# Norm sums in column groups, a narrow reciprocal spread by matmuls, and an earlier place for the filter spectra

## The reference

```python
def rmsnorm(x, g):
    xf = x.astype(jnp.float32)
    y = xf * lax.rsqrt(jnp.mean(xf * xf, axis=-1, keepdims=True) + EPS)
    return (y * g.astype(jnp.float32)).astype(x.dtype)

h = modulate(rmsnorm(x, norm1_g[l]), shift, scale)     # h * (1 + scale) + shift
P = h @ w_in[l]       # q, k, v, the Hyena inputs and two gates
# then attention, Hyena, merge, w_o; x += gate1 * ...
h = modulate(rmsnorm(x, norm2_g[l]), shift2, scale2)
# layer 0: dense SwiGLU (ffn_w1, ffn_w3, ffn_w2); layer 1: top-2 of 8 experts
```

## Time and profile before

| what | value |
|---|---|
| median of three runs | 1837.5 us |
| profiled execution, its own time | 1836.34 us |
| span of the profiled execution | 1834.5 us |
| mean granted TensorE clock | 0.988 |
| TensorE matmul busy | 1766.9 us, 96% of the span |
| VectorE, ScalarE, GpSimd busy | 38%, 23%, 3% |

### The profile page before, as it was taken

The page is one execution under the profiler, slowest core; times in us unless marked ns, Lnnn a source line. Parts: engine busy times, 40 slices in busy tenths (PEclk is TensorE's granted clock), DMA queues, the critical chain, the costliest instruction groups (busy, mean ns, idle before and its releaser), DMA issues.

```text
span 1834.5 us, 41948 instructions
## 1 busy us (share of the span) xinstructions
PE 1766.9 (96%) x19374; PEld 1398.8 (76%) x19374; DVE 696.2 (38%) x950; ACT 423.4 (23%) x582; POOL 52.9 (3%) x61
## 2 busy tenths in 40 slices
PE   7999999999999999998998999999999999999997
PEld 3777676786788888877877886778679997677775
DVE  5457656444433335978745552010100010101013
ACT  4233344332422222215324441000000000000001
POOL 0000000002000001210000010000000000000000
PEclk9999999999999999999999999999999999999998
DMA  9721311235122225773331389999999999999991
GB/s 390 298 93 46 108 58 47 69 117 221 69 91 91 91 96 205 254 293 113 126 108 70 138 352 367 382 418 403 389 398 405 411 405 400 374 405 399 420 410 68
DMA packets 66414, 440.26 MB, mean 240 GB/s; under 512 B 7537, under 2 KB 7793, under 8 KB 22850
## 3 DMA queue, kind: packets, MB, share of 16 engines
q1 hardware_dynamic: 60482, 404.19, 56.4%
q0 software_dynamic: 4976, 30.70, 4.5%
q10 hardware_dynamic: 784, 2.75, 0.4%
HBM read 433.81 MB, written 3.80 MB: 239 GB/s over the span
## 4 chain that ended last, share of the span: by engine, by line
PE 89%; DVE 6%; ACT 2%; issue 2%; DMA 0%; DVEq 0%; ACTq 0%; SPq 0%
PE psum L2082 25%; PE psum L1601 14%; PE psum L1603 13%; PE psum L1602 13%; PE psum L2103 12%; PE psum L1648 1%; PE psum L1840 1%; PE psum L1862 1%; ACT units_hi L632 1%; PE psum L2058 1%; DVE units_lo L1005 1%; PE psum L1631 1%; PE psum L1822 1%; PE psum L1823 1%; PE psum L1824 1%
## 5 line engine op out<-in xcount | busy, mean ns | idle before, releaser
L2082 PE MATMUL psum<-expert_units,gathered 128*32 128x256 f32 (+1 forms) x9216 | 469.0, 361 | 3.8 <-issue 3.5
L2082 PEld LDWEIGHTS psum<-expert_units,gathered 128*32 128x32 f32 x9216 | 366.0, 110 | 99.4 <-issue 6.6
L1601 PE MATMUL psum<-h_hi,units_hi 128*128 128x512 f32 (+1 forms) x928 | 344.7, 371 | 10.9 <-DVE h_lo L1076 5.3
L1603 PE MATMUL psum<-h_hi,units_lo 128*128 128x512 f32 (+1 forms) x928 | 336.6, 363 | 0.0
L1602 PE MATMUL psum<-h_lo,units_hi 128*128 128x512 f32 (+1 forms) x928 | 336.5, 363 | 0.0
L1005 DVE TENSOR_TENSOR units_lo<-raw_units,units_hi 128x2048 fp32r<-128x2048 f32 (+2 forms) x88 | 175.2, 1991 | 265.9 <-ACT units_hi L632 265.9
L632 ACT ACTIVATE units_hi<-raw_units 128x2048 fp32r<-128x2048 f32 (+2 forms) x88 | 147.2, 1673 | 406.3 <-PE psum L1603 351.3
L2103 PE MATMUL psum<-expert_units,expert_midT 128*32 128x256 f32 x4080 | 229.6, 379 | 0.1
L1601 PEld LDWEIGHTS psum<-h_hi,units_hi 128*128 128x128 f32 x928 | 176.9, 191 | 50.8 <-issue 22.4
L2103 PEld LDWEIGHTS psum<-expert_units,expert_midT 128*32 128x32 f32 x4080 | 172.5, 110 | 50.5 <-issue 2.3
L1603 PEld LDWEIGHTS psum<-h_hi,units_lo 128*128 128x128 f32 x928 | 176.8, 191 | 27.4
(11 more groups left out here) (307 smaller groups left out, 1688.5 us busy)
## 6 DMA issues: line engine op xcount, KB each, us to landing
expert_units<-in_moe_up SPq DMA_DIRECT2D x128, 1024.0 KB, 9.9
expert_units<-in_moe_w SPq DMA_DIRECT2D x88, 1024.0 KB, 9.7
expert_units<-in_moe_up_rest SPq DMA_DIRECT2D x64, 768.0 KB, 7.6
raw_units<-in_w_in SPq DMA_DIRECT2D x40, 1024.0 KB, 4.8
raw_units<-in_ffn_w SPq DMA_DIRECT2D x22, 1024.0 KB, 4.8
mod_units<-in_w_mod_rows POOLq DMA_DIRECT2D x20, 1024.0 KB, 6.2
raw_units<-in_ffn_w SPq DMA_DIRECT2D x16, 704.0 KB, 5.4
raw_units<-in_w_pab SPq DMA_DIRECT2D x16, 512.0 KB, 3.3
```

The costliest lines, as they stand in the source:

```text
L1601: MM(o, wh, xh, start=first, stop=False)
L1603: return MM(o, wl, xh, start=False, stop=last)
L2082: ins = MM(o[GRP * q:GRP * (q + 1), :], G[:, k, at, GRP * rr:GRP * (rr + 1)], W[:, kk, q, :], start=k == 0 and rr % 2 == 0, stop=k == DK - ...
```

## The change

Each norm sum becomes four matmuls with 32 columns of ones, one in each column group of TensorE. Group g sums a quarter of the tokens, so that PSUM rows 32g to 32g+31 hold the sums of quarter g in 128 columns (64 for q = 3). Root and reciprocal run over these 128 (64) columns. Four further matmuls (`norm_spread`) have a broadcast column of the identity as weights and lay row 32g over all 128 rows, for quarter g; ScalarE copies the result to `rs` (`norm_rows`). Whoever read `rs` after the reciprocal now waits for `n_rs`.

The order changes too. At the start sums 6 and 7 go ahead of the taps, the spread follows the taps, the first scale trip precedes all spectra, and all eight spectra precede the shift trip. VectorE's reciprocal goes ahead of the tap decays. ScalarE copies four spectra before unit 0's high part, and makes unit 1's after 12 of the 16 norm items. Only the 64 rows of `hy_w3` that layer 0 needs are loaded (256 KB in place of 512 KB). The two modulation trips after `w_o` are cut: two units before sums 6 and 7, two after them, then the spread.

```diff
@@ ScalarE
-                A(rs[:, c0:TOK], PS[:, 7, c0:TOK], ACT.Sqrt, bias=eps[:, 0:1], scale=1.0 / D).then_inc(n_rt, 1)
+                A(rs[:, norm_part(q, 0, c0)], PS[:, 7, norm_part(q, 0)], ACT.Sqrt, bias=eps[:, 0:1], scale=1.0 / D).then_inc(n_rt, 1)
+
+            def norm_rows(q):
+                c0 = norm_c0[q]
+                act.wait_ge(n_spread, q + 1)
+                A(rs[:, c0:TOK], PS[:, 7, c0:TOK], ACT.Copy).then_inc(n_rs, 1)
...
                     norm_root(0)
-                    for q in range(5):
+                    norm_rows(0)
+                    for q in range(4):
                         spectrum_out(0, q)
                     hi(0, 0, 0)
-                    for q in range(5, 7):
-                        spectrum_out(0, q)
-                    hi(1, 1, 0)
-                    early = 7
+                    early = 4
...
                     norm_root(2)
-                    for q in range(2, 5):
+                    for q in range(2, 4):
                         spectrum_out(l, q)
+                    norm_rows(2)
+                    spectrum_out(l, 4)
                     early = 5
...
+                else:
+                    norm_hi(0, SHIFT1, HH, 0, 12)
+                    hi(1, 1, 0)
+                    norm_hi(0, SHIFT1, HH, 12, 4)
@@ VectorE
-                link(V_.reciprocal(rs[:, c0:TOK], rs[:, c0:TOK]))
+                V_.reciprocal(rs[:, norm_part(q, 0, c0)], rs[:, norm_part(q, 0, c0)]).then_inc(n_rec, 1)
...
-                    decayed(0)
                     norm_reciprocal(0)
                     dve.wait_ge(consts_in, 16)
+                    decayed(0)
@@ TensorE
-                    MM(PS[:, 7, c0:TOK], ones[:], sq[:, k % 2, c0:TOK], start=k == 0, stop=k == DK - 1).then_inc(n_pe, 1)
+                    for g in range(4):
+                        last = MM(PS[GRP * g:GRP * (g + 1), 7, norm_part(q, 0)], ones[:, 0:GRP], sq[:, k % 2, norm_part(q, g, c0)],
+                                  start=k == 0, stop=k == DK - 1, skip_group_check=True)
+                    last.then_inc(n_pe, 1)
+
+            def norm_spread(q):
+                c0 = norm_c0[q]
+                pe.wait_ge(n_rec, q + 1)
+                for g in range(4):
+                    last = MM(PS[:, 7, norm_part(q, g, c0)], ident[:, GRP * g:GRP * g + 1].to_broadcast([P, P]), rs[:, norm_part(q, 0, c0)],
+                              start=True, stop=True)
+                last.then_inc(n_spread, 1)
...
+                    if l and q == 4:
+                        norm_spread(2)
                     if bank == 7:
-                        pe.wait_ge(n_rt, 2 * l + 1)
+                        pe.wait_ge(n_rs, 2 * l + 1)
...
+            norm_sums(0, range(6, DK))
             filter_taps(0)
-            norm_sums(0, range(6, DK))
-            filter_spectra(0, 0, 2)
+            norm_spread(0)
             pe.wait_ge(s_ready, 1)
             mod_units(0, 0)
-            filter_spectra(0, 2, 3)
+            filter_spectra(0, 0, 2)
             mod_turn(0, 0)
-            filter_spectra(0, 3, 6)
+            filter_spectra(0, 2)
             mod_units(0, 1)
-            filter_spectra(0, 6, 7)
             mod_turn(0, 1)
-            filter_spectra(0, 7)
...
+                mod_units(l, MTRIPS - 1, 0, 2)
                 norm_sums(2 * l + 1, (DK - 2, DK - 1))
+                mod_units(l, MTRIPS - 1, 2)
+                norm_spread(2 * l + 1)
                 if l == 0:
-                    mod_units(0, LATE_TRIP)
...
-            mod_units(1, MTRIPS - 1)
-            pe.wait_ge(n_rt, 4)
```

More of the change, by code:

```diff
@@ L314, in build @@
         n_sq, n_pe, n_rt = sem("n_sq"), sem("n_pe"), sem("n_rt")
+        n_rec, n_spread, n_rs = sem("n_reciprocal"), sem("n_spread"), sem("n_rs")
         n_add = sem("n_add")
@@ L378, in build, with norm_part @@
         pooled = [0, 6, 6, 6, 0, 0]
+        def norm_part(q, g, c0=0):
+            w = (TOK - norm_c0[q]) // 4
+            return slice(c0 + g * w, c0 + (g + 1) * w)
         adds_before = [sum(c - 1 for c in pooled[:q] if c) for q in range(6)]
@@ L732, in _ @@
                     spectrum_out(l, q)
-                    norm_hi(2 * l, SHIFT1, HH, 2 * (q - early), 2)
-                norm_hi(2 * l, SHIFT1, HH, 2 * (8 - early), DK if l else 2 * DK)
+                    if l:
+                        norm_hi(2, SHIFT1, HH, 2 * (q - early), 2)
+                if l:
+                    norm_hi(2, SHIFT1, HH, 2 * (8 - early), DK)
+                else:
+                    norm_hi(0, SHIFT1, HH, 0, 12)
+                    hi(1, 1, 0)
+                    norm_hi(0, SHIFT1, HH, 12, 4)
                 for n in range(U_U):
@@ L857, in _ @@
                 norm_root(2 * l + 1)
+                norm_rows(2 * l + 1)
                 if l == 0:
@@ L1079, in norm_lo @@
                 end = len(todo) if end is None else end
+                dve.wait_ge(n_rs, q + 1)
                 for j in range(first, end):
@@ L1627, in norm_sums, with mod_units @@
                         pe.wait_ge(n_add, adds_before[q] + pooled[q] - 1)
-                        MM(PS[:, 7, c0:TOK], ones[:], square_sum(q), start=True, stop=False).then_inc(n_pe, pooled[q])
+                        for g in range(4):
+                            last = MM(PS[GRP * g:GRP * (g + 1), 7, norm_part(q, 0)], ones[:, 0:GRP], square_sum(q)[:, norm_part(q, g)],
+                                      start=True, stop=False, skip_group_check=True)
+                        last.then_inc(n_pe, pooled[q])
                         continue
                     pe.wait_ge(n_sq, 8 * q + k + 1)
-                    MM(PS[:, 7, c0:TOK], ones[:], sq[:, k % 2, c0:TOK], start=k == 0, stop=k == DK - 1).then_inc(n_pe, 1)
-            def mod_units(l, i):
-                if l or i:
+                    for g in range(4):
[5 more added lines that the diff above has]
+                pe.wait_ge(n_rec, q + 1)
+                for g in range(4):
+                    last = MM(PS[:, 7, norm_part(q, g, c0)], ident[:, GRP * g:GRP * g + 1].to_broadcast([P, P]), rs[:, norm_part(q, 0, c0)],
+                              start=True, stop=True)
+                last.then_inc(n_spread, 1)
+            def mod_units(l, i, first=0, end=MRING):
+                if (l or i) and first == 0:
                     pe.wait_ge(md_row, trip(l, i))
                 rows = P // MRING
-                for u in range(MRING):
+                for u in range(first, end):
                     if l:
```

3 lines of the change are left out of this document (2 added, 1 removed).

## The result

The changed kernel takes 1842.79 us (median of 20 runs, 1839.52 to 1849.77), the kernel before 1839.47 us (20 runs, 1834.91 to 1843.32) in the same rounds. The ratio on record is 1.0028, 95% interval 1.0019 to 1.0036; it is not the quotient of the two medians, which is 1.0018. By the ratio the changed kernel is 5.2 us slower, by the medians 3.3 us, where the forecast was 3.9 us faster and its range ended at 1837.2 us. The profiled execution of the changed kernel took 1841.88 us (span 1840.1, before 1834.5), and TensorE still holds the chain of waits.

The account below looks back on a forecast made before the run. TensorE, holding 89% of the chain of waits, was taken to bound the kernel. Start -3.4, second norm -1.6, third 0 and fourth +1.1 gave -3.9 us, so 1832.4 profiled and 1833.6 median, range 1829.6 to 1837.2.

Parts of the forecast that it names:

- The start: First norm up to the first product: short sums and new order bring -3.4 us, product near 43.1 against 46.10.
- T: End of the taps at the start: 23.3 us forecast, 21.7 if never slow, about 25 if slow throughout.
- T + 18.9: Start of the first product, 18.9 us after the taps end: 42.2 us before any allowance for slow matmuls.
- the 0.9 added for slow matmuls there: Spread or scale trip after the one-column tap matmuls: 0.9 us for slow matmuls, first product at 43.1.
- a possible 1.6 us: Taps at the start: holes left by short sums make TensorE slow until half way, +1.6 us.
- Rival (b): Start: clock low throughout the taps and part of the trip; T near 25, product 45.5, total -1.1, 1836.4 us; chance 0.27.
- The second norm: Second norm: earlier sums and narrow reciprocal let VectorE start at 455.35 in place of 456.99, -1.6 us.
- The third: Third norm: -0.3 from down projection sums, +0.3 from the later last spectrum copy, sum 0.
- The fourth: Fourth norm: half trip and spread between sum and copy delay VectorE's first block and the router matmuls, +1.1 us.
- rival (c): Norm sums: column groups do not overlap, each sum costs 0.86 us and spreads come on top; 1837.5 us, chance 0.06.
- the row bound: Narrow norm sum: a record every 54 ns if the weight load binds, up to 0.43 us a sum.
- Rival (d): First product stays at 1.2 GHz for all 48 matmuls, 10 us more; with other gains +4.5, 1842 us; chance 0.06.

Follow-up runs that it names:

- e2_wide_sums: Changed kernel, new order kept, but first norm with 128-column sums, wide root and reciprocal, no spread; ratio 0.9992 to the kernel before.
- e3_fill: Changed kernel, narrow sums kept, plus eight extra 128x128 matmuls with unused result among the first norm's sums; ratio 0.9992 to the kernel before.
- e7_second_only: Kernel before with only the second norm made narrow as in the changed kernel; ratio 0.9987 to the kernel before.
- e10_first_expert: e2_wide_sums plus 80 repeats of the first expert's first four matmuls, result unchanged; ratio 1.0025 to the kernel before.
- c4_fourth_mix: c1_mix with a narrow fourth norm, its spread before the trip's last unit, and eight extra matmuls behind that unit; ratio 0.9966 to the kernel before.
- e4_fourth_old: Changed kernel with the fourth norm as before: 128-column sums, wide reciprocal, whole modulation trip behind the sums; ratio 1.0007 to the kernel before.
- c1_mix: Changed kernel's new start order and narrow second norm, with wide first and third norms and the fourth as before; 1832.16 us, ratio 0.9968 to the kernel before.
- e6_fourth_fill: Changed kernel plus eight extra 128x128 matmuls with unused result between the fourth norm's spread and the router; ratio 1.0012 to the kernel before.

## Why the prediction was wrong

**The start: the failing step.** "I expect it slow at the taps' start and raised half way", T = 23.3. It was not raised until 32.1 us, so T was 26.8, and spread and scale trip cost 2.01 and 5.23 us in place of 0.96 and 3.7. The rest of the working held: T + 18.9, with these 2.6 us in place of the 0.9 added for slow matmuls there, gives 48.3 against the 48.54 measured, and in e2_wide_sums, with T = 23.6 and no spread, 41.5 against 41.69. The term was -3.4 us and came out at +2.4. The prediction counted the short sums as a gain and their holes as a possible 1.6 us. The runs show the holes to be the larger matter: with eight extra matmuls in them the same kernel is 5.9 us earlier at its first product. Rival (b) had the mechanism but not its length: it put T near 25 and the product at 45.5.

Two readings of the rows were wrong on the way. TensorE was not busy without a break ahead of the taps before: there was the hole of 0.71 us. And the 3.61 us of the two sums behind the taps were not all work: four such records took 1.98 us at 12.05 us, and the clock was 0.50 there:

```profile
23.00:24.00 1.00, 1.00 (x3) 0.48 (x2) 0.96 (x2) 0.00 (x0) 0.00 (x0) 0.50 1.04 434
```

Moving the sums away therefore saves their work and leaves the slow stretch to whatever follows the one-column taps. The prediction gave 0.9 us for that; where the stretch came back, in e3_fill, it cost 1.7.

**The second norm:** -1.6 forecast, -1.63 in the trace of the changed kernel and of e7_second_only. **The third:** 0 forecast, from +0.3 at the norm and -0.3 in the down projection; measured +0.58 and -0.37. That a shorter reciprocal earns nothing behind ScalarE's copies was right. These two steps are forecasts that held by their mechanism.

**The fourth:** +1.1 forecast. The path was +0.5 (block from +2.63 to +3.16), TensorE's wait 1.59 us, and the remaining 4.2 us are the router's loop at 0.50. The prediction named the wait ("TensorE idle about 1 us before the router matmuls") and did not price the clock behind it. At the first products it had thought of that; at the router it had not.

**Prices.** One narrow sum of 128 columns took 0.43 us with its drain at the high clock (0.3 plus 0.17 predicted), the root 0.37, the reciprocal 0.95, the copy 0.60, the eight records of the spread 1.16 with drain (1.03 predicted). Column groups overlap, so rival (c) falls. The Trainium skill, page "TensorE: Matmul & The Clock Gate", section "LDWEIGHTS (loading the stationary operand)", leads to an estimate of 0.21 us for a sum without drain. The trace's 0.43 less the 0.17 taken for the drain is 0.26, nearer to it than to the row bound of 0.43.

**Sum.** In the trace: +2.44 at the start, -1.63 at the second norm, -0.37 in the down projection, +0.58 at the third norm, +1.59 in a slow stretch from 895.7 to 899.1 us that the kernel before did not have, +0.02 up to the fourth norm's entry, +0.53 to its block, +4.24 in the router's loop, -1.80 in the experts: +5.60. The 1.59 and the -1.80 are no effect of the change that the runs show: e2_wide_sums and e10_first_expert are the same up to the first expert, and only the second has the slow stretch near 890 us; and the stretch behind the logits scatters from -1.8 to +3.9 us. Rival (d) ended near the measured time, with 1842, by a mechanism that did not occur, so that was luck: at the first product the clock was low from 49.2 to 52.6 us, 3.4 us, where before 3.2 us of the product were slow. What hit the kernel was the same cost at two other places: the taps and what follows them, where rival (b) made it too small, and the router, which no rival named.

## What to carry to other kernels

Ahead of dense matmul work, a saving on TensorE that turns busy time into holes can cost more than it saves. Price the clock at each place where the new order leaves TensorE waiting, small waits included, and try a few useless matmuls in the hole: here eight of them were worth 6.6 us at the start and 2.9 at the router by the ratios, each uncertain by some 3 us, and 5.9 and 2.9 us in the traces. Fit them to the hole: in c4_fourth_mix they were too many and held the router up by 1.2 us. Shorten an operation only where the rows show somebody waiting for it: of four narrow norms only the second was shown to earn its cost, and two thirds of that came from shorter sums and root.

## What the runs showed of the hardware

Being busy did not by itself bring the clock back. In the changed kernel TensorE worked without a pause from 17 to 32 us at 1.2 GHz, on eight wide records of 64 rows, sixteen of one column, the spread and column-group matmuls. In e3_fill the same taps ran at the high clock from 16.57 us: the clock had risen at 11.7 us, among the sums and the extra matmuls. In all five profiles with the narrow sums unfilled it rose only between 30.7 and 32.8 us, in the other nine between 10.6 and 13.1 us. The Trainium skill, page "TensorE: Matmul & The Clock Gate", Part 1, describes the low clock as the state of rest that activity ends; these 15 us are a case where activity of such shapes did not end it. The one-column matmuls also took twice the time at 1.2 GHz (16 records in 3.21 us against 1.68). And a wait of 0.6 to 1.6 us ahead of the router's small matmuls was followed by a fall of the clock while they ran, in all seven profiles that have it, at once in four of them and after 2.7 to 3.5 us in three. In the seven where no wait stood ahead of them (among them the kernel before, e4_fourth_old and c1_mix) or useless matmuls filled it (e6_fourth_fill, c4_fourth_mix), it fell only behind them.
